# Two norms joined at a border, a reordered end, and low parts of split weights behind the attention steps of their mark

## The chip, the cores and the metric

The kernel runs on one core of one Trainium2 chip. The metric is device time in microseconds, here the median of three runs; a profiled execution of the same kernel gives the trace.

## What is computed

A transformer block of two layers is followed by a second block with its own weights. All of it works on 256 rows of 1024 fp32 values. Cut to what matters:

```
def first_block(x, mem, ...):                       # two layers
    for layer in range(2):
        h = rms_norm(x, norm_g[layer])
        proj = h @ w_in[layer]                      # heads of three kinds: sb, mb, mem
        ...                                         # attention of each kind, gated by silu
        mixed = concat([o_sb, o_mb, o_mem])
        x = x + mixed @ w_out[layer]                # "wo"
    return rms_norm(x, final_norm_g)                # the final norm of the first block

def second_block(x, meta_tokens, ...):
    h = concat([filler, meta, x])                   # 16 meta rows ahead of the 256
    u = rms_norm_2(h, pre_mix_gain)
    proj = u @ w_in_2                               # qa, ka, va, qb, kb, vb, gates
    o_swa  = windowed_gqa_sink_attention(...)       # 16 heads in 4 groups: "swa"
    o_diff = differential_attention(...)            # 8 heads: "diff"
    merged = g_swa * (o_swa @ w_branch_swa) + g_diff * (o_diff @ w_branch_diff)
    h = h + rms_norm_2(merged @ w_out, post_mix_gain)
    u = rms_norm_2(h, pre_ffn_gain)
    f = (silu(u @ w_gate) * (u @ w_up)) @ w_ffn_out
    return (h + rms_norm_2(f, post_ffn_gain))[128:]
```

At the border between the blocks two norms follow each other on the same rows: the final norm makes x, and the first norm of the second block makes its input xn of that x.

## The kernel before

**Tiling.** The 256 rows are two tiles, t=0 and t=1, of 128. A weight matrix is worked through in units: a unit is two chunks of 128 rows of the matrix by 512 columns (384 in swa and diff). For precision each fp32 operand is split into a high and a low part, and a unit does for each tile and chunk three matmuls: high x high, high x low, low x high. So a unit is six matmuls for t=0 (step `unit`) and six for t=1 (`unit_end`). Four units make a group, and each tile of a group adds up in one bank of PSUM.

**Weights.** SyncE loads a unit's raw weights into one of four raw buffers. ScalarE writes the high part (w_hi), VectorE the low part (w_lo = raw - w_hi). Both are one step, `split`, in the old kernel. A raw buffer is free, and its next load goes out, when its low part is written. The parts go into one of five slots (ten late in the kernel). A split is put into the order when the unit is less than SPLIT_AHEAD = 3 units ahead of the one that TensorE begins, and the slot's last user has ended.

**The order.** All engines walk one list of steps, STEPS, and each issues its own part of every step; semaphores hold them together. `make_plan` writes a timeline of units, norms and turns (transposes on TensorE), and `lay_out` makes the list of it. When the last unit of a head group has ended, the group's attention steps are put at marks, so many units later, by the table SLOTS: the key and query turns (turn_qk), scores, the softmax (soft), scale (VectorE divides the probabilities of a pair of heads by their sum; this is L1802), turn_p and turn_tm (transposes of the probabilities), out_t (times the values), mix_t (split of the result). A mark is half a unit. At each mark stand the matmuls of the half unit, the evacuation of a finished bank, the split (by kind of group ahead of or behind the attention steps) and the attention steps due. For head groups of swa and diff GpSimd rotates queries and keys (rope, L1128 to L1140) before turn_qk. Two small banks of PSUM are shared in a ring by turns and outs, so a turn or out can wait until the result of two turns ago has been read.

**The splits of turned operands.** A turn's result in PSUM is copied by ScalarE into a high part (h_hi, m_hi, mix_hi) and VectorE subtracts it into the low part (h_lo, m_lo, mix_lo, L1717 and L1807). The operand is ready with the low part.

**The border to swa.** After the last units of wo of layer 1 (a[3] and b[3] for the two halves of the columns) VectorE adds the bank to x. Then comes `norm` for x to x (the final norm) and `norm` for x to xn: each is ScalarE's square over 1024 columns with a sum (L1496), a logarithm and an exponential, and VectorE's scaling of the row by that and by the gain (L1706). xn is turned into h for t=0 and, after three units of swa, for t=1. Between them TensorE does a `meta` group: 8 chunks of weights meta_w with 16 meta rows (L1202). Its weights are loaded whole (two DMAs of 1 MB, L1017) when the meta group before has been read.

**The end.** After the last hidden group of the ffn, its product f is turned (turn_f) and split into m_hi and m_lo. ScalarE has to load another table of functions (`tables`, L1549) before the last norm. Four held units of w_ffn_out run for t=0 first, then the two last units, which need the new m_hi and m_lo.

## Time and profile before

| | |
|---|---|
| runs | 833.49, 833.73, 832.29 us |
| median | 833.49 us |
| the profiled execution | 831.91 us |
| its span, first to last instruction | 830.1 us |
| mean granted clock of TensorE | 0.995 |
| TensorE busy | 801.1 us, 97% |
| VectorE, ScalarE, GpSimd busy | 497.9, 467.8, 136.5 us |

A row of the timeline gives the start in us from the start of the span, the duration, the engine, the line, what is written and what is read, and in brackets the idle time just before and the engine that ended it. Matmuls are pipelined: one starts before the one in front of it has ended, so the distance of starts says what a matmul costs.

### The profile page before, as it was taken

The page shows a single profiled execution, that of the slowest core. Times are in us where ns is not written, and L with a number is a line of the kernel's source. Part 1 is how long each engine was busy: PE and PEld are TensorE (multiplying, and loading weights), DVE is VectorE, ACT ScalarE, POOL GpSimd, SP SyncE. Part 2 cuts the span into 40 slices and gives each one's busy share as a digit, 9 for nine tenths or more (in the row PEclk, how much of TensorE's full clock was granted, in tenths as well). Part 3 has the DMA queues.
Part 4 walks back from the last instruction along what each step waited for, and adds up shares of the span by engine and source line. Part 5 has one row for each costly group of instructions (what it writes and reads, how often), then busy time and mean ns, then how long its engine had stood idle before and what let it go on. Part 6 is the DMA issues. An engine that isn't in the chain of part 4 may idle for free.

```text
span 830.1 us, 12690 instructions
## 1 busy us (share of the span) xinstructions
PE 801.1 (97%) x4238; PEld 651.3 (78%) x4238; DVE 497.9 (60%) x731; ACT 467.8 (56%) x1004; POOL 136.5 (16%) x204
## 2 busy tenths in 40 slices
PE   7999999999999998899999999999999999999996
PEld 5887778887777885877778888778887888888885
DVE  5456565684566555666765767666787544555454
ACT  5677586475666555555566565654557433444352
POOL 2011021000243110434433546000000000000000
PEclk9999999999999999999999999999999999999999
DMA  8964553469764546442323435456775645465631
GB/s 237 285 174 145 151 169 104 144 190 286 228 203 128 190 152 197 138 123 85 89 77 96 128 116 164 128 178 228 244 230 160 203 151 179 153 203 191 209 133 51
DMA packets 147294, 137.78 MB, mean 166 GB/s; under 512 B 15024, under 2 KB 115648, under 8 KB 147232
## 3 DMA queue, kind: packets, MB, share of 16 engines
q1 hardware_dynamic: 145136, 129.89, 50.9%
q0 software_dynamic: 2096, 7.09, 3.1%
q8 instruction: 36, 0.59, 0.3%
q14 instruction: 26, 0.21, 0.1%
HBM read 135.90 MB, written 1.05 MB: 165 GB/s over the span
## 4 chain that ended last, share of the span: by engine, by line
PE 82%; ACT 5%; DVE 5%; POOL 4%; issue 3%; DMA 1%; DVEq 0%; SPq 0%; ACTq 0%; POOLq 0%
PE psum L1182 66%; PE psum L1160 7%; PE psum L1281 3%; PE psum L1416 3%; ACT w_hi L1463 2%; ACT probs L1590 1%; POOL rtmp L1128 1%; POOL rtmp L1130 1%; DVE w_lo L1659 1%; DVE probs L1802 1%; PE psum L1202 1%; POOL rtmp L1132 1%; PE psum L1342 1%; POOL stage L1134 1%; PE psum L1384 1%
## 5 line engine op out<-in xcount | busy, mean ns | idle before, releaser
L1659 DVE TENSOR_TENSOR w_lo<-raw,w_hi 128x1024 fp32r<-128x1024 f32 (+1 forms) x234 | 274.1, 1194 | 118.8 <-ACT w_hi L1463 83.4
L1182 PE MATMUL psum<-w_hi,h_hi 128*128 128x512 f32 (+1 forms) x656 | 259.9, 396 | 4.8 <-DVE w_lo L1659 2.2
L1463 ACT ACTIVATE w_hi<-raw 128x1024 fp32r<-128x1024 f32 (+1 forms) x234 | 230.9, 1011 | 41.0 <-PE psum L1182 17.2
L1182 PE MATMUL psum<-w_lo,h_hi 128*128 128x512 f32 (+1 forms) x656 | 247.2, 377 | 0.0
L1182 PE MATMUL psum<-w_hi,h_lo 128*128 128x512 f32 (+1 forms) x656 | 246.6, 376 | 0.0
L1182 PEld LDWEIGHTS psum<-w_hi,h_hi 128*128 128x128 f32 x656 | 124.1, 189 | 31.4 <-issue 14.8
L1182 PEld LDWEIGHTS psum<-w_lo,h_hi 128*128 128x128 f32 x656 | 123.9, 189 | 19.2
L1182 PEld LDWEIGHTS psum<-w_hi,h_lo 128*128 128x128 f32 x656 | 124.3, 190 | 15.4
L1182 PE MATMUL psum<-w_hi,m_hi 128*128 128x512 f32 x152 | 60.3, 397 | 1.2 <-DVE m_lo L1717 1.2
L1182 PE MATMUL psum<-w_lo,m_hi 128*128 128x512 f32 x152 | 59.3, 390 | 0.0
L1182 PE MATMUL psum<-w_hi,m_lo 128*128 128x512 f32 x152 | 59.2, 389 | 0.0
L1128 POOL TENSOR_TENSOR rtmp<-stage,cf 128x256 f32<-128x256 f32 (+2 forms) x36 | 30.3, 840 | 160.5 <-ACT stage L1525 128.7
L1182 PE MATMUL psum<-w_hi,mix_hi 128*128 128x512 f32 x128 | 52.9, 414 | 0.0
L1590 ACT ACTIVATE probs<-psum,stats 128x272 f32<-128x272 f32 (+2 forms) x104 | 47.1, 465 | 10.5 <-DVE stats L1787 6.0
L1182 PE MATMUL psum<-w_lo,mix_hi 128*128 128x512 f32 x128 | 50.2, 392 | 0.0
L1182 PE MATMUL psum<-w_hi,mix_lo 128*128 128x512 f32 x128 | 49.9, 390 | 0.0
L1505 ACT ACTIVATE m_hi<-psum 128x512 fp32r<-128x512 f32 (+1 forms) x27 | 14.4, 536 | 62.1 <-PE psum L1160 62.1
L1717 DVE TENSOR_TENSOR m_lo<-psum,m_hi 128x512 fp32r<-128x512 f32 (+1 forms) x27 | 16.4, 609 | 51.4 <-ACT m_hi L1505 51.4
L1608 ACT ACTIVATE p_t<-psum 128x512 f32<-128x512 f32 (+1 forms) x44 | 24.1, 566 | 27.8 <-PE psum L1160 27.7
L1518 ACT ACTIVATE stage<-psum 128x128 f32<-128x128 f32 (+1 forms) x52 | 15.6, 301 | 37.5 <-PE psum L1182 37.5
L1160 PE MATMUL psum<-cf,probs 128*128 128x128 f32 (+1 forms) x212 | 30.7, 274 | 4.1 <-DVE probs L1802 2.5
L1182 PEld LDWEIGHTS psum<-w_hi,m_hi 128*128 128x128 f32 x152 | 28.6, 188 | 7.1 <-issue 1.6
(171 smaller groups left out, 1001.1 us busy)
## 6 DMA issues: line engine op xcount, KB each, us to landing
raw<-in_w_in SPq DMA_DIRECT2D x112, 256.0 KB, 3.8
raw<-in_w_ffn_in SPq DMA_DIRECT2D x88, 256.0 KB, 4.1
raw<-in_w_in SPq DMA_DIRECT2D x24, 512.0 KB, 3.9
raw<-in_w_out SPq DMA_DIRECT2D x24, 512.0 KB, 3.5
raw<-in_w_in SPq DMA_DIRECT2D x64, 192.0 KB, 2.7
raw<-in_w_ffn_out SPq DMA_DIRECT2D x22, 512.0 KB, 4.2
meta_w<-in_w_in SPq DMA_DIRECT2D x10, 1024.0 KB, 7.9
raw<-in_w_mem_kv SPq DMA_DIRECT2D x8, 512.0 KB, 3.9
```

The source lines that it names most:

```text
L1128: nc.gpsimd.tensor_tensor(a, v[:, t, :, 0:w], ct[:, t].unsqueeze(1).to_broadcast(shape), ALU.mult)
L1160: last = nc.tensor.transpose(o, i, cf[0:n, C_ID:C_ID + n])
L1182: last = nc.tensor.matmul(psum[:, bank, 0:n], sx[name][:, c, t * P:(t + 1) * P], wx[:, kk, 0:n], start=u["first"] and kk == 0 and z == 0, ...
L1281: return nc.tensor.matmul(o, l, r, start=start, stop=stop, skip_group_check=True)
L1416: last = nc.tensor.matmul(dst, src[:, blk * P:(blk + 1) * P], vs[:, kt, v0:v0 + wide], start=(n == 0), stop=end)
L1463: nc.scalar.activation(weights(u)[0][:, :, 0:n], raw[:, u["raw"], :, 0:n], ACT.Copy)\
L1505: nc.scalar.activation(dst[0], src, ACT.Copy).then_inc(turned_hi, 1)
L1518: nc.scalar.activation(st[:, t, 0:K["qw"]], ps[:, 0:K["qw"]], ACT.Copy, scale=SCALE)
L1590: last = nc.scalar.activation(probs[:, j % 4, t, 0:n], src, ACT.Exp, bias=stt[:, t:t + 1], accum_out=stt[:, 2 + t:3 + t])
L1608: last = nc.scalar.activation(p_t[:, s["pt"] % 2, 0:n], psum[:, s["bank"], 0:n], ACT.Copy)
L1659: nc.vector.tensor_tensor(lo[:, :, 0:n], raw[:, u["raw"], :, 0:n], hi[:, :, 0:n].bitcast(F32), ALU.subtract)\
L1717: nc.vector.tensor_tensor(dst[1], src, dst[0].bitcast(F32), ALU.subtract).then_inc(turned, 1)
```

## The change

**Joined norms.** At the border the two norms become one chain. With y = x * gain of the final norm, X = mean(x^2) and Y = mean(y^2), the two factors multiply to (Y + eps (X + eps))^-1/2. The new steps: `row_scale` (VectorE writes y by halves of 512 columns into xn), `row_sum` (ScalarE squares a half of x and a half of y with their sums), `twin` (GpSimd adds the sums of x and makes the bias, ScalarE does one logarithm and one exponential, VectorE scales y by that and the second gain, in two halves, each with its own signal to the turns). x itself, the result of the final norm, is needed only much later; its two scalings now stand behind the fourth swa group.

**Meta weights** are loaded and waited for by halves, the first half as soon as the first four chunks of the group before were read; the meta group at the border is done in two halves around the first turn.

**swa's first group** has marks of its own, SLOTS["swa0"]: scores and softmax of its second pair half a unit later than in the other groups (6.95 for 6.45), and all that follows them too; turn_p of the first pair stays at 6.5. Its units for t=0 run all four before t=1 is turned.

**Low parts** are a step of their own, `split_lo`, which stands behind the attention steps of the mark in which the high part is made. High parts keep their places.

**The end**: one high part and the table load stand behind turn_f.

```diff
     "swa": dict(turn_qk=(3.25, 2.75), scores=(4.45, 4.45, 6.45, 6.45), soft=(4.95, 4.95, 6.95, 6.95),
...
+    "swa0": dict(turn_qk=(3.25, 2.75), scores=(4.45, 4.45, 6.95, 6.95), soft=(4.95, 4.95, 7.45, 7.45),
+                 scale=(5.95, 8.45), turn_p=(6.5, 6.5, 9, 9), turn_tm=(6.9, 9.4), out_t=(7.5, 10),
...
         while split < min(most, held) and split < begun + ahead and order[split]["before"] < ended:
             steps.append(("split", order[split]))
+            lows.append(order[split])
             split += 1
+
+    def low_parts(most):
+
+        while len(lows) > most:
+            steps.append(("split_lo", lows.popleft()))
...
         for k in sorted(k for k in due if k <= clock):
             steps.extend(due.pop(k))
         if g["kind"] in SPLIT_LAST:
+            low_parts(0)
             splits()
+        else:
+            low_parts(0)
...
         else:
-            final, after = norm(source="x", dest="x"), norm(source="x", dest="xn")
-            line.append(final[0])
-            line.extend(("unit_b", u) for u in (a[3], b[3]))
-
+            final, after = norm(source="x", dest="x", twin=True), norm("twin", source="x", dest="xn")
             metas.append(meta_group(4))
             metas[4]["evac_later"] = True
-            line.extend([after[0], ("meta", metas[4]), final[1]])
-            line.extend(norm_turns("xn", "h", 0))
-            line.append(after[1])
+            for us, g in ((a, outs[0]), (b, outs[1])):
+                line.extend([("unit_a", us[3]), row_scale(final, g, 0), row_sum(final, g, 0, "x"),
+                             row_sum(final, g, 0, "y")])
+            line.append(("hold", "begun"))
+            turns = norm_turns("xn", "h", 0)
+            line.extend([("unit_b", a[3]), row_scale(final, outs[0], 1), after[0], row_sum(final, outs[0], 1, "x")])
+            line.extend([("unit_b", b[3]), ("meta", metas[4], (0, KC // 2)), turns[0]])
+            line.extend([row_sum(final, outs[0], 1, "y"), row_scale(final, outs[1], 1)])
+            line.extend([("meta", metas[4], (KC // 2, KC)), ("hold", None), ("splits", "one"), ("hold", "begun"), turns[1]])
+            line.extend([row_sum(final, outs[1], 1, "x"), row_sum(final, outs[1], 1, "y"), after[1]])
...
         if kv == 0:
-            line.extend(("unit_a", u) for u in g["units"][:3])
-            line.extend(norm_turns("xn", "h", 1))
-            line.append(("unit_a", g["units"][3]))
-            line.extend(("evac", dict(g=metas[n], t=0)) for n in (3, 4))
-            line.extend(("unit_b", u) for u in g["units"])
+            us = g["units"]
+            us[3]["evac_later"] = True
+            line.extend(("unit_a", u) for u in us)
+            line.extend(norm_turns("xn", "h", 1) + [("evac", dict(g=g, t=0)), ("hold", None), ("splits", "one")])
...
+        elif kv == 3:
+            add(g)
+            line.extend(final)
...
-    line.append(("tables", None))
     held = outs_of(nf - 3) + outs_of(nf - 2)
-    line.extend(("unit_a", u) for u in held[:3])
-    line.append(("turn_f", dict(j=nf - 1, f=last_g)))
-    line.append(("unit_a", held[3]))
+    line.extend(("unit_a", u) for u in held[:2])
+    line.extend([("hold", "begun"), ("unit_a", held[2]), ("turn_f", dict(j=nf - 1, f=last_g))])
+    line.extend([("hold", None), ("splits", "one"), ("tables", None), ("unit_a", held[3])])
...
                     for i in range(2):
+                        if g["n"]:
+
+                            sp.wait_ge((meta_first, meta_done)[i], g["n"])
                         src = cols[i * 4 * P:(i + 1) * 4 * P, :].rearrange("(k p) n -> p k n", p=P)
-                        sp.dma_start(meta_w[:, 4 * i:4 * i + 4, :], src).then_inc(meta_landed, 16)
+                        sp.dma_start(meta_w[:, 4 * i:4 * i + 4, :], src).then_inc(meta_landed[i], 16)
...
+                elif what == "twin":
+                    N, t = s["norm"], s["t"]
+                    c = 4 * (N["n"] % 4) + 2 * t
+                    Y1 = hsum[:, 7 + 4 * t:8 + 4 * t]
+                    rs = nstat[:, 16 + c:17 + c]
+                    act.wait_ge(row_bias, t + 1)
+                    act.wait_ge(row_summed, 4 * t + 4)
+                    link(nc.scalar.activation(rs, Y1, ACT.Ln, bias=twins[:, t:t + 1]))
+                    nc.scalar.activation(rs, rs, ACT.Exp, scale=-0.5).then_inc(rstd_ready, 1)
```

What it moves, at three places. First VectorE at the border, from the addition of the first wo half to x up to the low parts of h for t=1. Before:

```order
L1878 TENSOR_TENSOR x<-x,psum 128x512
L1659 TENSOR_TENSOR w_lo<-raw,w_hi 128x2x384
L1878 TENSOR_TENSOR x<-x,psum 128x512
L1659 TENSOR_TENSOR w_lo<-raw,w_hi 128x2x384
L1706 SCALAR_TENSOR_TENSOR x<-x,nstat,gain 128x1024
L1878 TENSOR_TENSOR x<-x,psum 128x512 x2
L1706 SCALAR_TENSOR_TENSOR xn<-x,nstat,gain 128x1024
L1706 SCALAR_TENSOR_TENSOR x<-x,nstat,gain 128x1024
L1717 TENSOR_TENSOR h_lo<-psum,h_hi 128x4x128 x2
L1706 SCALAR_TENSOR_TENSOR xn<-x,nstat,gain 128x1024
```

Now, from the low parts of two swa units on:

```order
L1764 TENSOR_TENSOR w_lo<-raw,w_hi 128x2x384 x2
L2001 TENSOR_TENSOR x<-x,psum 128x512
L1805 TENSOR_TENSOR xn<-x,gain 128x512
L2001 TENSOR_TENSOR x<-x,psum 128x512
L1805 TENSOR_TENSOR xn<-x,gain 128x512
L2001 TENSOR_TENSOR x<-x,psum 128x512
L1805 TENSOR_TENSOR xn<-x,gain 128x512
L1814 SCALAR_TENSOR_TENSOR xn<-xn,nstat,gain 128x512 x2
L2001 TENSOR_TENSOR x<-x,psum 128x512
L1840 TENSOR_TENSOR h_lo<-psum,h_hi 128x4x128
L1805 TENSOR_TENSOR xn<-x,gain 128x512
L1764 TENSOR_TENSOR w_lo<-raw,w_hi 128x2x384
```

The whole-row scalings in a chain are gone; each half of x is followed at once by its product with the gain, and xn of t=0 is scaled in two halves before the last half of x is even added.

Second TensorE in the third swa group's units, where the first group's attention lies: qk and cb are the scores of its second pair, "cf,probs 128x128" is turn_p of the first, "cf,probs 16x128" turn_tm. Before:

```order
L1281 MATMUL psum<-qk 128x272 x4
L1281 MATMUL psum<-cb 128x128 x4
L1160 MATMUL psum<-cf,probs 128x128 x8
...
L1160 MATMUL psum<-cf,stage 128x128 x2
L1160 MATMUL psum<-cf,gates 128x16
L1160 MATMUL psum<-cf,probs 16x128 x4
```

Now:

```order
L1229 MATMUL psum<-cf,probs 128x128 x8
...
L1229 MATMUL psum<-cf,stage 128x128 x2
L1229 MATMUL psum<-cf,gates 128x16
L1229 MATMUL psum<-cf,probs 16x128 x4
L1353 MATMUL psum<-qk 128x272 x4
L1353 MATMUL psum<-cb 128x128 x4
```

The scores moved behind six matmuls of a unit and two turns, and turn_p is now the first of them.

Third VectorE in the head group mb 1 of layer 0, where o_st is the result of a mem head. Before:

```order
L1717 TENSOR_TENSOR m_lo<-psum,m_hi 128x4x128
L1659 TENSOR_TENSOR w_lo<-raw,w_hi 128x1024
L1835 RECIPROCAL rec<-stats 128x2
L1844 SCALAR_TENSOR_TENSOR o_st<-psum,rec,sgate 128x64 x2
L1717 TENSOR_TENSOR m_lo<-psum,m_hi 128x4x128
```

Now:

```order
L1840 TENSOR_TENSOR m_lo<-psum,m_hi 128x4x128
L1958 RECIPROCAL rec<-stats 128x2
L1967 SCALAR_TENSOR_TENSOR o_st<-psum,rec,sgate 128x64 x2
L1764 TENSOR_TENSOR w_lo<-raw,w_hi 128x1024
L1840 TENSOR_TENSOR m_lo<-psum,m_hi 128x4x128
```

The low part went behind the result of the head and in front of the next low part of a turned operand.

## Rows read from the trace of the kernel before

**Rows 1.** The page: its first line and TensorE's busy time.

```profile
span 830.1 us, 12690 instructions
...
PE 801.1 (97%) x4238; PEld 651.3 (78%) x4238; DVE 497.9 (60%) x731; ACT 467.8 (56%) x1004; POOL 136.5 (16%) x204
```

**Rows 2.** TensorE's waits by releaser: us in total, times, longest.

```profile
PE psum L1160 <- DVE probs L1802: 2.5, 6, 1.0
...
PE psum L1160 <- DVE o_st L1844: 1.5, 2, 1.2
```

**Rows 3.** Timeline of TensorE at the border.

```profile
320.76 0.47 PE L1182 MATMUL psum<-w_hi,mix_hi 128*128 128x512 f32 x1
...
328.77 1.91 PE L1202 MATMUL psum<-meta_w,meta_s 128*16 128x512 f32 x16 [2.29 <-DMA meta_w<-in_w_in]
331.42 1.06 PE L1160 MATMUL psum<-cf,xn 128*128 128x128 f32 x8 [0.73 <-DVE xn L1706]
333.73 0.41 PE L1182 MATMUL psum<-w_hi,h_hi 128*128 128x384 f32 x1 [1.25 <-DVE h_lo L1717]
...
338.49 1.04 PE L1160 MATMUL psum<-cf,xn 128*128 128x128 f32 x8
...
340.70 0.41 PE L1182 MATMUL psum<-w_hi,h_hi 128*128 128x384 f32 x1
```

**Rows 4.** Stretches: busy us (instructions) per engine, then granted clock.

```profile
334.00:337.50 3.50, 3.50 (x13) 3.50 (x12) 2.70 (x4) 2.17 (x6) 0.55 (x2) 0.51 0.49 154
341.00:346.00 5.00, 5.00 (x31) 5.00 (x30) 4.15 (x8) 3.63 (x8) 2.89 (x5) 1.00 0.32 83
```

**Rows 5.** Meta weights: the group before's first matmuls, the DMA issues, their landing.

```profile
318.32 1.05 PE L1202 MATMUL psum<-meta_w,meta_s 128*16 128x512 f32 x8
...
L1017 SPq DMA_DIRECT2D meta_w<-in_w_in x2: 368/438/509, 320.8 to 321.2; - x2
...
DMA to landing us min/median/max: 5.2/6.4/7.5
```

**Rows 6.** Groups of VectorE by form (busy, mean ns), and a square in ScalarE's timeline.

```profile
L1878 DVE TENSOR_TENSOR x<-x,psum 128x512 f32<-128x512 f32 x8 | 5.3, 683 | 3.7 <-PE psum L1182 3.7
...
L1706 DVE SCALAR_TENSOR_TENSOR x<-x,nstat,gain 128x1024 f32<-128x1024 f32 x2 | 2.6, 1284 | 1.3 <-ACT nstat L1499 1.3
...
814.57 0.60 ACT L1474 ACTIVATE p_t<-psum 128x512 f32<-128x512 f32 x1 [3.59 <-PE psum L1182]
```

**Rows 7.** Timelines of GpSimd, VectorE and TensorE around swa's first rope.

```profile
345.83 4.39 POOL L1128 TENSOR_TENSOR rtmp<-stage,cf 128x320 f32<-128x320 f32 x1 [1.78 <-ACT stage L1521]
...
345.94 3.54 DVE L1659 TENSOR_TENSOR w_lo<-raw,w_hi 128x768 fp32r<-128x768 f32 x4
...
352.54 0.44 PE L1160 MATMUL psum<-cf,stage 128*128 128x128 f32 x2 [1.13 <-POOL stage L1140]
```

**Rows 8.** Timeline of TensorE: second scores and first turn_p of swa.

```profile
363.82 1.19 PE L1281 MATMUL psum<-qk 64*128 64x272 f32 x8 [1.20 <-ACT stats L1594]
...
365.56 1.06 PE L1160 MATMUL psum<-cf,probs 128*128 128x128 f32 x8 [0.22 <-DVE probs L1802]
```

**Rows 9.** Timelines of VectorE and TensorE in two head groups of layer 0.

```profile
137.75 1.23 DVE L1659 TENSOR_TENSOR w_lo<-raw,w_hi 128x1024 fp32r<-128x1024 f32 x1 [3.85 <-ACT w_hi L1463]
...
72.13 0.85 PE L1416 MATMUL psum<-stage,probs 128*128 128x64 f32 x6 [0.55 <-DVE m_lo L1717]
```

**Rows 10.** Timeline of TensorE: the last turn_p of a group's second pair.

```profile
433.60 1.06 PE L1160 MATMUL psum<-cf,probs 128*128 128x128 f32 x8 [0.95 <-DVE probs L1802]
```

**Rows 11.** Timelines of TensorE and ScalarE at the end.

```profile
812.93 0.47 PE L1182 MATMUL psum<-w_hi,m_hi 128*128 128x512 f32 x1 [1.21 <-DVE m_lo L1717]
...
806.24 1.28 ACT L1549 ACT_TABLE_LOAD   x1
807.54 2.96 ACT L1463 ACTIVATE w_hi<-raw 128x1024 fp32r<-128x1024 f32 x3
810.40 0.57 ACT L1505 ACTIVATE m_hi<-psum 128x512 fp32r<-128x512 f32 x1
```

More of the change, by code:

```diff
@@ L196, in lay_out @@
     free, user = deque(range(NSLOT)), {}
-    for what, arg in timeline:
+    for what, arg, *_ in timeline:
         if what == "more_slots":
@@ L240, in part @@
         if g["kind"] in SPLIT_LAST:
+            low_parts(0)
             splits()
-    for what, arg in timeline:
+        else:
+            low_parts(0)
+    for what, arg, *rows in timeline:
         if what == "splits":
-            splits(split + 1 if arg == "one" else arg)
+            splits({None: len(order), "one": split + 1}.get(arg, arg))
+            low_parts(0)
         elif what == "hold":
@@ L276, in lay_out @@
             steps.append((what, arg))
-    assert not due and begun == ended == split == len(order)
+    assert not due and not lows and begun == ended == split == len(order)
     return steps
```

125 lines of the change are left out of this document (106 added, 19 removed).

## Prediction

> **What bounds the kernel now.** I read the page first. TensorE is busy for 801.1 of 830.1 us [rows 1], so no edit that leaves its matmuls alone can return more than the 29 us in which it is idle, plus what its clock lost. The change keeps every matmul; it moves them and what feeds them. So the question at each place is which wait of TensorE ends last there. The profiled execution took 831.91 us, 1.8 over its span, and is 1.6 below the median of the runs, 833.49; I make the sum against 831.91 and add 1.6 at the end.
>
> The waits of TensorE by releaser come next: no single one is large. The longest sum is 2.5 us in 6 waits for VectorE's scaled probabilities; another is 1.5 in 2 for o_st [rows 2]. The timeline of TensorE shows where the others lie. At the border to swa (from the last wo matmul, which ends at 328.77 - 2.29 = 326.48, to the first t=1 matmul of swa at 340.70) it waits 2.29 us for meta weights, 0.73 for xn and 1.25 for h_lo [rows 3], 4.27 us in all. Behind these waits the granted clock is 0.51 for 3.5 us, which is the lower of its two levels, 1.2 GHz [rows 4]. Work that ran 3.5 us there would have taken 3.5 x 0.51 = 1.8 at 2.4 GHz, so 1.7 us more are lost. The matmul counts agree: 13 in 3.5 us against 31 in 5.0. The border loses 6.0 of its 14.2 us.
>
> **The border.** Three things are done to it. *Meta weights:* two DMAs were issued at 320.8 and 321.2 and landed 5.2 and 7.5 us later, at 326.0 and 328.7 [rows 5]; the matmuls waited for both. Now each half waits only for its own readers and has its own semaphore. The first four matmuls of group 3 end at 318.32 + 1.05 = 319.4 [rows 5], so half 0 can go out at about 319.6 and land by 325, and half 1 still goes out at about 320.8, behind a queue 1 us shorter, and lands at about 327.4. The four matmuls of half 0 take half of 1.91 [rows 3], from 326.5 to 327.4, and do not wait.
>
> *Joined norms:* before, ScalarE's square and its two small steps, VectorE's scaling of x, and the same again for xn ran one behind the other. Now the squares of x and of x*gain are summed by halves while the last wo units run. VectorE adds a half to x in 0.683 [rows 6]; the product with the gain has no row, and I take 0.65 for it, between half a low part, which also has two SBUF inputs (1.23 for 1024, so 0.62 [rows 9]), and a scaling of a whole row, 1.28 [rows 6]. ScalarE's square of 512 is 0.60 [rows 6]; with its sum read out behind it I take 0.7. The chain for t=0: the four half units from 320.76 to 326.48 [rows 3] are 1.4 apart, so a's half leaves TensorE at 322.2 and b's at 323.6; a's is in x at 323.3 (two low parts are now queued in front of it) and b's at 324.6, and the four squares end at about 326.1. GpSimd's three 128x1 operations have no row: from nothing, under the last square, to 4.39 if one is locked out like the rope's [rows 7]; I take 0.7, ending at 326.3, since they are far smaller than that. Logarithm and exponential end at 326.9, and the first half of xn is there at 327.6. TensorE gets there at 327.4: it waits 0.2 to 0.5, and again nothing for the second half, which lies under meta's second four matmuls. h_lo of the first half is ready near 329.5, as the turns end near 329.6; the 1.25 is gone. Without gaps of that length the clock should hold.
>
> *What is late next:* t=1. Its turns now stand behind all four swa units of t=0, with only themselves as cover. Before, 2.2 us passed from the start of the turns (338.49) to the first t=1 matmul (340.70) [rows 3], and a unit of 6 matmuls at 0.17 (1.0 us) lay inside; now nothing does, so about 1.1 us of new wait. Border: 6.0 - 0.3 - 1.1 = **4.6 us** gained; from 2 (half 1 late and the clock down again) to 5.7.
>
> **swa's first head group.** *Rope:* GpSimd's multiply took 4.39 us while VectorE ran four low parts of 3.54 in a row, and TensorE then waited 1.13 for the rope's copy [rows 7]. The four are now spread: three stand before the first meta sum, two between the two sums and one behind. The cover from the last swa unit to this turn stays three units. I take **0.9** of the 1.13, with 0 and 1.13 as ends. The Trainium skill (SBUF — State Buffer, section "SBUF: two separate sides") says that a VectorE operation with two SBUF inputs and a GpSimd operation that reads SBUF lock each other out for a whole instruction; by that rule two low parts in a row cost the rope 1.8 us, and if they stay in its way this term is 0. The row of 4.39 beside 3.54 agrees with it.
>
> *Scores and turn_p:* before, the second pair's scores waited 1.20 for the first pair's softmax, ran 1.7, and turn_p then waited 0.22 for the scaled probabilities [rows 8]. The new slot 6.95 puts the scores half a unit behind, but turn_p keeps 6.5 and comes first. It needs the scaling, which ended at about 365.4 and does not depend on those scores. TensorE reaches it at 363.82 - 1.20 = 362.6. So it waits up to 365.5 - 362.6 = 2.9, less about 0.6 since the maximum no longer stands behind a low part: 2.3 in place of 1.42. The scores then wait for nothing. That is **-0.8**; +1.1 if the chain to the scaling were shortened as far, -1.5 at worst.
>
> *Final norm of x:* its two VectorE operations, 1.284 each [rows 6], move behind the mark of the last swa group, between mix_lo and the next maximum. They delay that softmax by up to 2.57. How much of it TensorE sees depends on the slack of this chain, which has no row: its turn_p waits are 0.2 to 1.0 before [rows 2], so there is none at its end, but matmuls of two units lie in it. I take a third, **-0.8**, with 0 and -2.57 as ends. Its six small ScalarE operations I cost at nothing, since ScalarE waits there for TensorE's transposes; without that cover they cost up to 0.3 each, half of a 512 square [rows 6].
>
> **Low parts behind the steps of their mark.** A low part takes 1.23 us with 1024 columns. Where one stood in front of a step that TensorE waits for, the wait goes: 1.5 in two waits for o_st [rows 2], the longer, 1.2, behind the w_lo at 137.75 [rows 9]; 0.95 at 433.60 [rows 10], where I count 0.9; and half of the other five waits for the probabilities (2.5 - 0.95 = 1.55), those of the groups' first pairs, 0.8. Where the part now comes in front of something else, a wait grows: at 72.13 TensorE waits 0.55 for m_lo [rows 9], and a low part now runs in front of that m_lo: -1.1. In layer 0 the norm of mem and the turn of the memory keys get a low part in front of them in the same way; TensorE waits for both already, and I count 0.4 each. Sum: 1.5 + 0.9 + 0.8 - 1.1 - 0.8 = **+1.3**. Waits that now are just covered and will show can't be read from the trace; I leave them to the range (-3 to +1). I cost late low parts at nothing for the matmuls: none of the waits here is for w_lo, two or three units are split ahead, and a part moves by less than a half unit.
>
> **The end.** TensorE reaches the units that need m_lo at 812.93 - 1.21 = 811.7 and waits 1.21. ScalarE had put a table load (1.28) and three high parts (2.96, up to 810.5) in front of m_hi, which ran from 810.40 for 0.57 [rows 11]; VectorE made the third low part behind the third high part, to about 812.1, and m_lo behind that. Now table load and third high part are behind m_hi. The turn has ended by 810.4, so m_hi ends at 811.0 or before and m_lo, as long as a sum of 512 at 0.683 [rows 6], at 811.7. The third high part ends at 812.0 and its low part at 813.2; the unit that wants it comes one half unit, 1.4, behind 811.7. So at most 0.1 is left at each: **+1.1**, from 0.6 to 1.2. The table load ends at about 813.3, as the first square is due, which has the whole of t=1 as cover.
>
> **Sum:** 4.6 + 0.9 - 0.8 - 0.8 + 1.3 + 1.1 = 6.3 us. 831.91 - 6.3 = 825.6, and with 1.6 for the median **827.2 us**.
>
> **Rivals.** (1) *The border gives half.* Half 1 of meta shares the wires with three weight loads and lands at 329, the gaps add up and the clock falls again: border 2.3, time 829.5, range 829 to 831. For: before, the fall came at 334 behind gaps like these; against: there they were 4.27 us. Chance 0.17. (2) *swa0 and the low parts help everywhere,* as they are meant to: +1.1 instead of -0.8, final norm free, 1 more from low parts: 6.3 + 1.9 + 0.8 + 0.5 = 9.5, 824.0, range 821.5 to 825. Chance 0.18. (3) *Slower.* Low parts pushed in front of turned parts, as at 72.13, cost 1.1 at each such mark. I count one for certain; the sum turns at 6.3/1.1, some 6 more such marks in the head groups of both layers, and by 9 of them the time is 833.5 + 3 = 837. Chance 0.07. For: layers 0 and 1 have 14 head groups with the same steps; against: most turned parts there aren't waited for at all now. (4) *No change:* new waits at three or four marks eat the border, 833. Chance 0.08.
>
> **How the numbers follow.** My forecast, 825 to 829, has 0.50. A measurement of this kernel tells about 0.2%, 1.7 us, from no change. Faster by more: forecast, (1) and (2), 0.85; within: 0.08; slower: 0.07. Leaving out (3), most of (4) and the low edge of (2) keeps 0.8 within 822.5 to 831.5.
>
> **What would show it.** Right: no wait for meta_w, the clock at 1.00 from 334 on, a wait for h_lo of about 1 us at the first t=1 unit of swa; a wait for the probabilities of about 2.3 us at the first turn_p of swa; none over 0.3 for o_st, at the place of 433.60 and at that of 812.93; about 1.6 at that of 72.13. Wrong: a wait for meta_w over 1 us or a clock of 0.5 in the border; waits for m_lo, mix_lo or sbt in more than three head groups.

## Result and profile after

The changed kernel took 834.42 us in the median of 20 runs (832.76 to 835.93), the kernel before 833.11 (830.69 to 834.03, also 20 runs). The ratio is 1.0022, with an interval of 1.0015 to 1.0029: slower by 0.2% (1.3 us by the medians, 1.8 by the ratio), where 6.3 us of gain had been forecast and 822.5 was the low, 831.5 the high end of the range. The profiled execution spans 832.4 us, against 830.1 in [rows 1]:

```profile
span 832.4 us, 12731 instructions
...
PE 800.0 (96%) x4238; PEld 650.4 (78%) x4238; DVE 501.5 (60%) x737; ACT 469.7 (56%) x1014; POOL 137.4 (17%) x210
```

TensorE's waits by releaser (us in total, times, longest), which answer to [rows 2], say where to look. The scaled probabilities were 2.5 us in six waits and are 4.4 in four; the blended ones of diff (L1945) and p_t are new, and m_lo in front of L1488 has grown from 0.5:

```profile
PE psum L1229 <- DVE probs L1925: 4.4, 4, 2.4
PE psum L1229 <- DVE probs L1945: 3.1, 5, 1.5
...
PE psum L1229 <- ACT p_t L1713: 2.2, 1, 2.2
...
PE psum L1488 <- DVE m_lo L1840: 1.7, 1, 1.7
```

**The border** did what it was made for, though less of it. No wait for meta_w is left, and the granted clock is 1.00 in the stretches of [rows 4], where it was 0.51 in the first. What answers to the three waits of [rows 3] is one for xn and, one tile later, one for h_lo. TensorE's timeline and the stretches:

```profile
328.30 0.63 PE L1229 MATMUL psum<-cf,xn 128*128 128x128 f32 x4 [1.22 <-DVE xn L1814]
...
337.12 0.41 PE L1251 MATMUL psum<-w_hi,h_hi 128*128 128x384 f32 x1 [1.17 <-DVE h_lo L1840]
```

```profile
334.00:337.50 3.50, 2.33 (x17) 2.09 (x16) 2.24 (x4) 1.96 (x5) 0.94 (x2) 1.00 0.42 122
341.00:346.00 5.00, 5.00 (x31) 5.00 (x30) 4.89 (x6) 3.46 (x6) 3.93 (x5) 1.00 0.73 192
```

**Swa's first head group.** TensorE's timeline, where [rows 8] had 1.20 and 0.22, and ScalarE's ahead of the second wait:

```profile
360.73 1.06 PE L1229 MATMUL psum<-cf,probs 128*128 128x128 f32 x8 [2.38 <-DVE probs L1925]
...
377.62 0.60 PE L1229 MATMUL psum<-cf,probs 128*16 128x128 f32 x4 [2.24 <-ACT p_t L1713]
```

```profile
374.92 0.49 ACT L1695 ACTIVATE probs<-psum,stats 128x272 f32<-128x272 f32 x1 [3.88 <-DVE stats L1897]
...
376.97 1.09 ACT L1713 ACTIVATE p_t<-psum 128x512 f32<-128x512 f32 x2
```

The first wait is the forecast 2.3. The second nobody had priced: the copy of the second pair's turned probabilities (p_t) now stands on ScalarE behind the four exponentials of the next group, which run from 374.92 on.

**Swa's fourth group.** VectorE runs the two scalings of x in front of the maximum (the reduction, L1891), and TensorE waits twice:

```profile
393.44 3.09 DVE L1829 SCALAR_TENSOR_TENSOR x<-x,nstat,gain 128x1024 f32<-128x1024 f32 x2
...
396.46 1.28 DVE L1891 TENSOR_REDUCE stats<-psum 128x4 f32<-128x1088 f32 x1
```

```profile
401.60 1.19 PE L1353 MATMUL psum<-qk 64*128 64x272 f32 x8 [0.91 <-ACT stats L1699]
...
404.68 1.94 PE L1229 MATMUL psum<-cf,probs 128*128 128x128 f32 x8 [1.56 <-DVE probs L1925]
```

The eight transposes at 404.68 take 1.94 us, where they take 1.06 at 360.73. The stretches say why (the granted clock is the figure in front of the last two): 1.00 behind the wait of 2.38, and 0.50, the lower level, behind these two.

```profile
360.00:363.00 3.00, 2.27 (x17) 2.10 (x17) 2.32 (x3) 1.40 (x3) 0.00 (x0) 1.00 0.17 43
...
404.00:407.00 3.00, 2.32 (x10) 2.35 (x11) 2.86 (x5) 0.94 (x2) 0.00 (x0) 0.50 0.22 77
```

**Low parts.** In layer 0 the wait of 0.55 in [rows 9] is 1.66, with a low part in front of m_lo, as forecast. In diff a low part stands in front of the reciprocals with which the blended probabilities begin, and its neighbours on VectorE and TensorE are:

```profile
71.36 1.22 DVE L1764 TENSOR_TENSOR w_lo<-raw,w_hi 128x1024 fp32r<-128x1024 f32 x1
...
73.33 0.85 PE L1488 MATMUL psum<-stage,probs 128*128 128x64 f32 x6 [1.66 <-DVE m_lo L1840]
```

```profile
510.19 1.22 DVE L1764 TENSOR_TENSOR w_lo<-raw,w_hi 128x1024 fp32r<-128x1024 f32 x1
...
512.51 1.62 DVE L1945 SCALAR_TENSOR_TENSOR probs<-probs,rec 128x272 f32<-128x272 f32 x2
...
514.28 0.84 PE L1229 MATMUL psum<-cf,probs 128*128 128x128 f32 x6 [1.47 <-DVE probs L1945]
```

**The end.** The wait of 1.21 in [rows 11] is gone; m_lo is there before the unit that wants it:

```profile
814.18 0.69 DVE L1840 TENSOR_TENSOR m_lo<-psum,m_hi 128x512 fp32r<-128x512 f32 x1 [1.37 <-ACT m_hi L1610]
...
815.02 0.47 PE L1251 MATMUL psum<-w_hi,m_hi 128*128 128x512 f32 x1
```

**Where the time went.** Both kernels issue 2808 matmuls with split weights. I number them in order and compare when the same number starts in the two traces; a step in the difference is a gain or loss at that place. In us, minus is a gain:

| place | forecast | traced |
|---|---|---|
| start (up to 25 us) | 0 | -0.3 |
| layer 0: 62.8, 73.3, 95.6 | +1.9 | +0.4 +1.1 +0.4 |
| layer 0: 130 | 0 | +0.4 |
| o_st waits, layers 0 and 1 | -1.5 | -1.4 -1.0 |
| border | -4.6 | -3.2 |
| rope of swa's first group | -0.9 | -0.7 |
| first group, first pair | +0.8 | +0.5 |
| first group, second pair | 0 | +2.2 |
| fourth group (final norm) | +0.8 | +3.4 |
| the other swa turns, up to the last | -1.7 | -1.6 |
| diff | 0 | +2.3 |
| gates and after | 0 | +0.7 |
| end | -1.1 | -1.1 |
| sum | -6.3 | +2.1 |

The spans differ by 2.3. Of diff's 2.3, 0.6 (a wait of 0.87 at 486.58) is in no other trace with these low parts. A trace is one execution: the same order of instructions starts up to 1 us earlier or later in another, and the clock can fall at another place (see the last section), so a step of this table is firm where a second trace repeats it.

### The profile page after: what moved, and what is told of

The parts are those of the page before. It is cut to its first block, busy times and chain, and to the rows that moved or that the text cites. A ratio compares the mean times of both kernels' runs of the same rounds, so it can differ in the third digit from the quotient of the medians.

```text
span 832.4 us, 12731 instructions
## 1 busy us (share of the span) xinstructions
PE 800.0 (96%) x4238; PEld 650.4 (78%) x4238; DVE 501.5 (60%) x737; ACT 469.7 (56%) x1014; POOL 137.4 (17%) x210
## 4 chain that ended last, share of the span: by engine, by line
PE 87%; DVE 5%; ACT 4%; issue 3%; DMA 1%; SPq 0%; POOL 0%; ACTq 0%; DVEq 0%; POOLq 0%
PE psum L1251 68%; PE psum L1229 7%; PE psum L1353 4%; PE psum L1488 3%; DVE w_lo L1764 2%; PE psum L1456 1%; ACT w_hi L1535 1%; PE psum L1414 1%; PE psum L1272 1%; ACT probs L1695 1%; DMA gain<-in_norm_g 1%; DVE probs L1925 0%; PE psum L1491 0%; DMA raw<-in_w_in 0%; PE psum L1416 0%
## 5 line engine op out<-in xcount | busy, mean ns | idle before, releaser
L1229 PEld LDWEIGHTS psum<-cf,probs 128*128 128x128 f32 (+1 forms) x212 | 23.4, 133 | 16.1 <-issue 10.1
```

The lines of the kernel that those rows point to most:

```text
L1229: last = nc.tensor.transpose(o, i, cf[0:n, C_ID:C_ID + n])
```

## The experiments

All ratios are to the kernel before, which ran on the same chip beside it. The changed kernel's own is 1.0022. The difference of two such ratios is uncertain by 1 to 1.6 us, so a difference near 1 us needs the trace beside it.

**Each part undone.** First the low parts, right behind their high parts again:

```diff
-            lows.append(order[split])
+            steps.append(("split_lo", order[split]))
```

> The changed kernel, with each low part back right behind its high part; all else as changed. Theory 1 (losses at single places): the low parts' move cost 0.4 + 1.1 + 0.4 us in layer 0 (waits at 62.8, 73.3, 95.6), about 2.3 in diff (waits for the blended probabilities, up to 1.47 at 514.28) and 1.0 in the four gates groups, and gave 1.4 at the o_st wait of layer 0, 0.5 in layer 1 and 1.5 in the last swa attention. Undone, the sum is about 1.7 us less than the changed kernel: 832.7, and the wait at the fourth turn of probabilities in diff falls from 1.47 to under 0.2. Theory 2 (the low parts are the whole loss): 829 or below, with the waits around swa's first and last head groups gone too. Theory 3 (swa's attention chain is the bound there, and the 4 us won at the border are waited off again whatever the order): 832 to 834, and waits in swa grow by what goes elsewhere.

Measured: 1.0076 (1.0060 to 1.0092), 4.5 us slower than the changed kernel instead of 1.7 faster. Outside swa each place came back about as named: 0.4, 1.1, 0.4 and 0.4 us regained in layer 0, 1.4 and, in layer 1, 0.9 lost at and behind o_st, the wait of 1.47 in diff gone. In swa it lost 3.5 us at the first turn of probabilities and 1.3 at the third:

```profile
353.29 1.44 DVE L1764 TENSOR_TENSOR w_lo<-raw,w_hi 128x768 fp32r<-128x768 f32 x1 [1.66 <-ACT w_hi L1535]
...
354.65 1.28 DVE L1891 TENSOR_REDUCE stats<-psum 128x4 f32<-128x1088 f32 x1
```

```profile
361.83 1.94 PE L1229 MATMUL psum<-cf,probs 128*128 128x128 f32 x8 [3.22 <-DVE probs L1925]
...
378.28 1.07 PE L1229 MATMUL psum<-cf,probs 128*128 128x128 f32 x8 [1.46 <-DVE probs L1925]
```

With a low part in front of the maximum the wait is 3.22 instead of 2.38. That is 0.8 of the 3.5; the rest is the clock, which is at the lower level from 361 to 367:

```profile
361.00:364.00 3.00, 2.17 (x10) 2.20 (x11) 2.43 (x3) 1.20 (x3) 0.00 (x0) 0.50 0.06 16
364.00:367.00 3.00, 3.00 (x13) 2.16 (x11) 0.44 (x1) 0.41 (x1) 0.00 (x0) 0.50 0.85 244
```

So theory 1 held at the places that it named, but its sum did not, since it had left out swa's first group; theory 2 fell. With swa's new marks the low parts' move keeps the maximum free. How much of the clock's 2.7 us every execution pays is not shown: the spans of the six runs go from 834.0 to 837.9 us.

Second, swa's first group on the common marks:

```diff
-    for what, places in SLOTS["swa0" if g.get("kv") == 0 else g["kind"]].items():
+    for what, places in SLOTS[g["kind"]].items():
```

> The changed kernel, with swa's first head group on the marks of the other swa groups (second pair at 6.45 again, all behind it half a unit earlier). Theory 1: the wait of 2.38 us for the first turned probabilities becomes one of about 1.4 at the scores and the turn together, and the wait of 2.24 us of the second pair's turn for ScalarE's copy of the transposed probabilities goes: 3 us less, 831.4. Theory 2 (low parts): no more than 0.5 us. Theory 3 (the chain is the bound): the 2.24 goes but the next turn of probabilities waits as much more; no change, 834.

Measured: 0.9979 (0.9970 to 0.9989), 3.6 us less than the changed kernel. The scores wait 0.64 and the turn 0.22; the wait for p_t is gone:

```profile
360.73 1.19 PE L1353 MATMUL psum<-qk 64*128 64x272 f32 x8 [0.64 <-ACT stats L1699]
...
362.46 1.06 PE L1229 MATMUL psum<-cf,probs 128*128 128x128 f32 x8 [0.22 <-DVE probs L1925]
```

Theory 1 stands, theory 3 falls: nothing behind waited longer.

Third, the final norm of x taken out of swa:

```diff
-        elif kv == 3:
-            add(g)
-            line.extend(final)
...
-        add(pl.group("bswa", ...))
+        us = pl.group("bswa", ...)["units"]
+        line.extend([("unit_a", us[0]), final[n], ("unit_b", us[0])])
+        line.extend(("unit", u) for u in us[1:])
```

> The changed kernel, with the two scalings of x by the final norm moved from behind swa's fourth group to the two branch groups bswa, one each, behind a half unit in which ScalarE and VectorE stand idle. Theory 1: the waits of 0.91 for stats and 1.56 for the probabilities at 401 to 405 us and the lower clock behind them (0.83 over 400 to 410) go, and nothing new waits in bswa: 3.4 us less, 831.0. Theory 2: no more than 0.5. Theory 3: waits in swa's second half stay at 2 us or more; 834.

Measured: 0.9983 (0.9970 to 0.9995), 3.2 us less than the changed kernel; 4.0 at this place in the trace, where both waits at the fourth group are gone and the clock is 1.00 from 400 to 410 (0.83 in the changed kernel). Theory 1 stands.

Fourth, the old end:

> The changed kernel with the old end (table load and all three high parts in front of the last turn of the ffn's product). All theories: the wait of 1.2 us for m_lo in front of the last units comes back, 1.1 us more, 835.5. If the end's gain is only moved to the tail, no change.

Measured: 1.0036 (1.0021 to 1.0051), 1.2 us more, which by itself is within the noise; but the wait of 1.21 for m_lo is back at 814.58, and the trace loses 1.0 us there and no more behind it. The term of the end was right.

**One part alone.** The border, with everything else of before (final norm in the bswa groups):

> The border done alone: the joined norms, the order of meta and of swa's first units, and the halves of the meta weights; the low parts, swa's first marks and the end are as before, and the final norm of x stands in the two bswa groups, where it cost nothing. Theory 1 (single places): the border gains 3.9 us by the trace of the changed kernel, and nothing is given back, so the ratio to the kernel before is 0.9953. Rival (given back): with the low parts in front of the attention steps, TensorE comes 4 us early to a chain of VectorE that is no earlier, and waits at the first head group's scores or probabilities for 2 us or more: 0.998 to 1.

Measured: 0.9961 (0.9948 to 0.9973), 3.2 us. The gain at the border is not given back in swa. The trace has 3.8 us up to 355 and loses 1.0 of them at a new wait in bswa: the final norm does cost something there, against what was expected. It comes up again below.

The low parts alone:

> The low parts' move done alone, with the old border, the old marks and the old end (the meta weights' halves have their own signals). By single places read from the changed kernel's trace: layer 0 loses 0.4 + 1.1 + 0.4 + 0.4 and gains 1.4, layer 1 gains 0.5 to 0.8, the swa attention gains 1.0 to 1.6, diff loses about 1.7 and gates 1.0. Sum: 1.2 to 1.6 us slower, ratio 1.0015 to 1.002. If the move is worth in the old order what it was worth in the changed one (5.0 us), it is 0.994.

Measured: 1.0003 (0.9988 to 1.0018). In the old order their move is worth nothing that can be told, and the gains and losses of the table come back (layer 0 the same four, diff +1.3 at one turn, the last turn of swa -1.0). The trace also loses 2.1 us at swa's first rope, with a wait of 1.77 for GpSimd (1.13 before) and a clock of 0.50 from 353 to 356; m_border_old below, which has the same order up to there, waits 1.07 and keeps the clock, so I don't count that as a price of the low parts. Their worth of 4.5 us in the changed kernel is for the most part worth against the new marks.

The old border in the changed kernel (the final norm stands at the border again, as it did):

> The changed kernel with the old border (two norms one behind the other, meta in one piece, swa's first units in the old order); low parts, swa's first marks and the end as changed. If the border is worth in the changed kernel what it is worth alone (0.9961 against the kernel before, 3.2 us), this one is 3.2 us above the changed one: ratio to the kernel before 1.006. If the border's gain was given back in swa, because TensorE came early to a chain that was no earlier, it is within 1 us of the changed kernel: 1.001 to 1.0035.

Measured: 1.0033 (1.0015 to 1.0051). I had overlooked that this also takes the norm out of swa. The trace shows both: 3.5 us lost at the border and the rope, 4.0 regained at the fourth group. As a package, the joined norms with the scalings put off into swa bring nothing that can be told (1.0033 against 1.0022, with intervals that overlap), while the border alone, with the scalings in bswa, brings 3.2.

**The two waits of the first group told apart:**

```diff
-scale=(5.95, 8.45), turn_p=(6.5, 6.5, 9, 9), turn_tm=(6.9, 9.4)
+scale=(5.95, 8.45), turn_p=(6.97, 6.97, 9, 9), turn_tm=(6.98, 9.4)
```

> The changed kernel with the first pair's turned probabilities of swa's first head group behind the second pair's scores, at the same mark (they stood in front of them); the second pair's marks stay. It tells the two waits of this group apart. Theory 1: the wait of 2.38 us falls to about 1, as 1.3 us of scores and six matmuls lie under it, and the wait of 2.24 us for ScalarE's copy stays whole, since the second pair's softmax is still half a unit late: 1.2 us less than the changed kernel. Rival: both waits are one chain and the second shrinks too, 3 us less.

Measured: 1.0035 (1.0021 to 1.0049), no gain. The first wait fell as expected, and the second grew:

```profile
362.27 1.09 PE L1229 MATMUL psum<-cf,probs 128*128 128x128 f32 x8 [1.07 <-DVE qk L1853]
...
375.92 0.61 PE L1229 MATMUL psum<-cf,probs 128*16 128x128 f32 x4 [2.73 <-ACT p_t L1713]
```

By the count of weight matmuls 1.7 us are won up to the second wait and 2.0 lost at and behind it. Neither expectation had it. Of the 2.0 only 0.5 is the longer wait, 2.73 for 2.24: ScalarE's exponentials, on which it hangs, began 1.7 us earlier too (373.21 for 374.92; this trace starts 0.4 earlier), so that chain followed TensorE for the most part. The other 1.5 is the clock, which stayed at 1.00 behind the wait of 2.24 and is at its lower level for a part of these two stretches behind that of 2.73:

```profile
376.00:379.00 3.00, 3.00 (x16) 2.12 (x18) 1.75 (x4) 2.25 (x4) 0.00 (x0) 0.67 0.20 58
379.00:382.00 3.00, 3.00 (x18) 1.70 (x16) 1.17 (x2) 0.38 (x1) 0.00 (x0) 0.77 0.44 131
```

The mean clock of the five runs is 0.993, that of the changed kernel's twenty 0.995, so on the whole it was lower in them; that the longer wait is the reason is not shown.

**The cures.** Low parts behind the attention steps only where that helped, the common marks, the norm in bswa:

```diff
             lows.append(order[split])
+            if not late:
+                low_parts(0)
...
+        late = g["kind"] in ("mb", "mem") and begun > 24 or g["kind"] == "swa" or g.get("d", 9) < 2
```

> All the cures together: the changed kernel with swa's first group on the old marks, the final norm of x in the bswa groups, and the low parts behind the attention steps only where that helped (swa, the first two diff groups, and the mb and mem groups but for the first), right behind their high parts elsewhere. Theory 1, by places: 3.0 less for the marks, 2.8 to 3.4 for the norm, 2.2 in layer 0, 1.9 in diff and 1.0 in gates less: 11 us below the changed kernel, ratio to the kernel before 0.989. If gains are given back down the line, 0.994 or more.

Measured: 823.09 us, against 831.18 for the kernel before beside it, ratio 0.9898 (0.9885 to 0.9912); by the ratios that is 10.3 us below the changed kernel, where 11 had been expected. It beats both. The sum over places held, with misses both ways: the marks and the norm gave 3.8 and 3.9 in the trace, layer 0 gave 1.4 for 2.2, and a new wait (below) cost 1.1.

The first of the edits alone, in the changed kernel:

> The changed kernel with one edit: low parts behind the attention steps only in swa, the first two diff groups, and the mb and mem groups but for the first; right behind their high parts elsewhere. By the single places 2.2 us in layer 0, 1.5 to 1.9 in diff and 1.0 in gates come back: 4.4 to 5.1 us below the changed kernel, ratio to the kernel before 0.9965 to 0.9970. If what is won early is waited off at swa, whose marks are unchanged here, ratio 1.000 or more.

Measured: 0.9979 (0.9969 to 0.9989), 3.6 us, some 1 less than expected. Diff and gates came back about as named (1.7 and 0.9). Of the 2.2 in layer 0 the trace has 1.3: the three places of the table gave 1.9, the fourth kept its wait of 0.2, and TensorE waits for o_st again, 0.36 at 142.62, which costs 0.6. And the clock fell at other places, behind the waits of 2.38 and of 2.24, which are as long as in the changed kernel, and held behind those of 0.92 and 1.56:

```profile
361.00:364.00 3.00, 3.00 (x16) 1.88 (x16) 0.44 (x1) 0.70 (x2) 0.00 (x0) 0.61 0.84 244
...
378.00:381.00 3.00, 3.00 (x16) 2.28 (x16) 2.48 (x4) 1.57 (x3) 0.00 (x0) 0.60 0.13 37
...
402.00:406.00 4.00, 1.95 (x16) 1.47 (x17) 2.55 (x5) 1.35 (x5) 0.00 (x0) 1.00 0.71 229
```

By the count of matmuls each fall costs 1.3 to 1.5 us (+1.5 and +1.3 against the changed kernel, and -1.3 at the fourth group). Two falls in place of one make this execution slower, but they don't explain the missing 1 us of the median: the mean clock of the eleven runs is 0.995, as in the changed kernel's twenty, and that of the profiled one 0.993. What layer 0 did not give back is about as much as is missing.

**Why the fourth group cost 4 us.** The same two scalings one unit later, behind the group's softmax:

```diff
-        elif kv == 3:
-            add(g)
-            line.extend(final)
...
-        add(pl.group("diff", ...))
+        us = pl.group("diff", ...)["units"]
+        line.extend([("unit", us[0])] + (final if d == 0 else []))
+        line.extend(("unit", u) for u in us[1:])
```

> The changed kernel with one edit: the final norm's two scalings of x stand one unit later, behind the softmax of swa's fourth group (in the changed kernel they are in front of its maximum). Work and amount are the same. Place theory: what cost 4.0 us was that 3.1 us of VectorE stood in front of the maximum, from which scores, exponentials, scaling and turn hang. Here their factors come behind the group's exponentials on ScalarE (about 400) and the two scalings end near 403.2, 1.1 us behind the time at which the probabilities' scaling began before: the turn waits about 1.3 us in all, the scores not at all, and 2.7 us of the 4.0 come back: ratio to the kernel before 0.999. Amount theory (VectorE has no room for 2.6 us in swa, wherever): 3 us or more are lost again, ratio 1.002.

Measured: 1.0013 (1.0004 to 1.0023), 0.7 us less than the changed kernel, which is within the noise; the trace regains 0.5 of the 4.0 us at this place. That number is the amount theory's (3 us or more lost again, 1.002) and not the place theory's (2.7 back, 0.999).

```profile
398.45 2.48 DVE L1828 SCALAR_TENSOR_TENSOR x<-x,nstat,gain 128x1024 f32<-128x1024 f32 x2 [2.54 <-ACT nstat L1587]
```

```profile
403.02 1.94 PE L1228 MATMUL psum<-cf,probs 128*128 128x128 f32 x8 [1.82 <-DVE probs L1924]
```

But VectorE stood idle for 2.54 us ahead of the scalings, waiting for factors that ScalarE makes behind the exponentials, so it did have room for them and the amount theory's reason does not hold either. In their new place they stand in front of the probabilities' scaling, again in the chain maximum, exponential, scaling, turn. One wait of 1.82 took the place of 0.91 and 1.56, and the clock fell as before (0.83 from 400 to 410). The place theory had said a wait of 1.3 and had left out the clock, which make up its miss. What the runs show is that the scalings cost 3.3 to 4.0 us by the traces at either place in this chain, against c_norm_late, where they stand outside of it.

**The wait of 0.84 us in the cured kernel.** GpSimd's, VectorE's and TensorE's timelines of h_sel at the rotation of the last diff head:

```profile
509.60 1.47 DVE L1831 SCALAR_TENSOR_TENSOR x<-x,nstat,gain 128x1024 f32<-128x1024 f32 x1
...
509.95 1.44 POOL L1203 TENSOR_TENSOR rtmp<-stage,cf 128x128 f32<-128x128 f32 x1
...
512.25 0.44 PE L1231 MATMUL psum<-cf,stage 128*128 128x128 f32 x2 [0.84 <-POOL stage L1205]
```

> All cures, with the final norm's first scaling moved once more, from the first bswa group, where GpSimd still rotates the last diff head (its multiply took 1.44 us beside the scaling, 0.46 to 0.65 without it, and TensorE then waited 0.84 for it), to the second, and the second scaling to the first gates group; no rotation runs there. Expected: the wait of 0.84 goes to about 0.2, 0.7 to 0.9 us less than with both in the bswa groups: ratio to the kernel before 0.989. If the operation of VectorE was not what slowed GpSimd, no change: 0.9898.

Measured: 0.9942 (0.9930 to 0.9954), 3.7 us slower than h_sel. The 0.84 went, but a wait nobody had in mind came: the second scaling, which ends at 544.9, holds the buffer of the gain, the gates' bias is loaded into it only then (issued at 545.43, landed 5.1 us later), and TensorE waits for the first gates bank.

```profile
551.42 0.47 PE L1253 MATMUL psum<-w_hi,h_hi 128*128 128x512 f32 x1 [3.63 <-DVE gates L2006]
```

> As h_sel (ratio 0.9898), with both scalings of x in the second bswa group, one unit apart: behind the last rotation, and in front of the gates, so that the buffer of the gain is free in time for the gates' bias (in the gates group it was not: TensorE waited 3.6 us). Expected: the wait of 0.84 for the rotated head goes, and no wait for the bias: 0.8 us less than h_sel, ratio 0.9889. If VectorE's scaling isn't what slows the rotation: 0.9898.

Measured: 823.84 us, 0.9894 (0.9878 to 0.9911), the same as h_sel. The 0.84 is gone here too, and no wait for the bias came; instead the second scaling delays the blended probabilities, for 1.2 us:

```profile
534.59 0.85 PE L1231 MATMUL psum<-cf,probs 128*128 128x128 f32 x6 [0.63 <-DVE probs L1947]
...
536.33 0.47 PE L1253 MATMUL psum<-w_hi,h_hi 128*128 128x512 f32 x1 [0.89 <-DVE xn L2010]
```

**The wait for xn.** One swap at the border, on top of h2_norm_later:

```diff
-row_scale(final, outs[0], 1), after[0], row_sum(final, outs[0], 1, "x")])
+after[0], row_scale(final, outs[0], 1), row_sum(final, outs[0], 1, "x")])
```

> As the run before, and at the border VectorE's product for the first half of t=1 stands behind the scaling of xn for t=0 instead of in front. In the changed kernel's trace this product (325.94 to 326.63) ran beside GpSimd's last addition for the bias, which took 0.70 us where the two others took 0.2, and the chain to xn waited for it; TensorE waits 1.22 us for xn. Expected: the addition takes 0.2, the wait falls by 0.5 to about 0.7, 0.5 us less: ratio 0.9884. If the product costs as much in its new place (the next low parts of h behind it), no change.

Measured: 0.9943 (0.9929 to 0.9956), as without it (0.9942; the 0.9884 expected was reckoned before h2_norm_later had missed). GpSimd's addition took 0.19 and the wait for xn fell by 0.5 as expected, and 0.37 came for h_lo, as the second alternative had it:

```profile
326.65 0.63 PE L1231 MATMUL psum<-cf,xn 128*128 128x128 f32 x4 [0.68 <-DVE xn L1816]
...
329.22 0.41 PE L1253 MATMUL psum<-w_hi,h_hi 128*128 128x384 f32 x1 [0.37 <-DVE h_lo L1842]
```

## Why the prediction was wrong

The terms that rested on a wait seen in the trace of before had the right sign, and most of them the right size. Those for work put into a place where nothing waited yet did not, and they are all on the losing side: the final norm of x, swa's second pair and the waits that were "just covered" are 7.2 us off together, of 8.4 in all. The step that failed is to price such work at nothing or at a third.

**The border** (4.6 said, 3.2 traced). The mechanism was right: no wait for meta_w, no low clock. The size was off by 1.4. The chain to xn was the step: TensorE waited 1.22 us for it instead of 0.2 to 0.5. "GpSimd's three 128x1 operations" were taken as 0.7 us; they took 0.20, 0.19 and 0.70 one after another, each with its way to the next, and ended at 326.7 instead of 326.3, and TensorE came 0.3 earlier than forecast (327.1). The wait of about 1.1 for h_lo at t=1 was forecast and is 1.17. Some 0.4 of the 1.4 lies in no wait and stays open.

**Swa's first marks** (0.8 said, 2.7 traced). The first pair's wait was right (2.3 said, 2.38 measured). What I did not do is to follow the second pair: I priced the slot of its scores and not the marks of all that follows them, though the change names them. Its turn_p moved half a unit, past the softmax of the next group, and on ScalarE the copy of p_t then stands behind four exponentials. The order lists would have shown it. b_swa0_old, which puts the common marks back, is 3.6 us faster.

**The final norm of x** (0.8 said, 3.4 traced). "I take a third" was the failed step, and c_norm_late shows what it was worth (3.2 us). The two operations lasted 3.09 us and not 2.57, since GpSimd rotated beside them, and the chain behind them had no slack: TensorE waited 0.91 + 1.56 against 0.28 before, 2.2 us more, and the lower clock added 1.3 (from n_sel, where the same waits without it cost that much less). Even the end of the range that I gave, 2.57, was too small, since it priced the delay and not the clock.

**Low parts** (gain of 1.3 said, loss of 1.3 traced). The named places were right to 0.2 us, the o_st wait of layer 0 and those of [rows 9] and [rows 10] among them, but for layer 1: its o_st wait was 0.3, and 1.0 was gained at and behind it. A wait that was not named, in layer 0, cost 0.4. But "waits that now are just covered" was left to the range. They are 1.7 us in diff, where the part went from in front of m_lo, which nobody waits for, to in front of the blended probabilities, and 0.7 in the gates groups, where it went between the two evacuations of a bank. This is rival (3)'s mechanism, and other steps than the turned parts that it names. It also left out what the move is good for: with swa's new marks it keeps the wait of 2.38 from being one of 3.22 and the clock from falling there (a_lo_old is 4.5 us slower in all; the fall is seen in one execution).

**The end** (1.1 said, 1.1 traced, 1.2 by the run that undoes it) and **the rope** (0.9 said, 0.7 traced) held.

**Slips in the sums**, which change little: 2.3 in place of 1.42 is 0.9 and not 0.8; the scores' "1.7" includes the wait of 0.22; that wait is counted in the 1.42 and again among the five other waits of the low parts; rival (2) speaks of 1 more from low parts and adds 0.5.

**Rivals.** None was it. I gave the border half (1) and all help (2) more than a third of the chance and slower 0.07, with a single mechanism. The range missed because its upper end, 831.5, lay beside that of rival (1), which halves one term. The low ends that I had given to the six terms (2, 0, -1.5, -2.57, 1.3 - 3 and 0.6) add up to a loss of 3.2 us: that sum should have stood beside the chance of 0.07.

## What to carry to other kernels

When a step moves in an in-order kernel, list for each engine what it passes and what now stands behind it, through the whole chain, and price each new neighbour at its full time until a row shows slack; zero is the best case, and a wait seen before is only where the gains are. Where a chain such as maximum, exponential, scaling and turn is already waited for at its end, any operation put into it costs most of its time, wherever in the chain it is put, and the clock may fall behind the longer wait. When an edit shortens one wait and brings nothing in all, look at the next one in both traces: how much longer it is, and what the granted clock is behind it. In f_turnp7 the first was 0.5 us and the second 1.5.

## What the runs showed of the hardware

**GpSimd beside VectorE.** An addition of 128x1 on GpSimd takes 0.19 us; the one that ran beside VectorE's product of two SBUF inputs took 0.70. GpSimd's and VectorE's timelines of the changed kernel:

```profile
325.72 0.19 POOL L1139 TENSOR_SCALAR eps_col<-eps_col 128x1 f32<-128x1 f32 x1
325.99 0.70 POOL L1140 TENSOR_TENSOR eps_col<-eps_col,hsum 128x1 f32<-128x1 f32 x1
```

```profile
325.94 0.69 DVE L1805 TENSOR_TENSOR xn<-x,gain 128x512 f32<-128x512 f32 x1
```

It ended when VectorE's did, at 326.7. The rotation's multiplies of 128x128 took 0.45 to 0.66 in most places of the changed kernel, 1.17 to 1.27 in ten that ran beside a low part, and 1.44 in h_sel beside the scaling of x. So the expectation of h2_norm_later had only the short ones in view. It goes the other way as well: the two operations on the blended probabilities took 1.62 at 512.51 and 1.47 at 484.96 (in front of the wait of 0.87) with GpSimd rotating, 0.91 elsewhere. The Trainium skill (SBUF — State Buffer, section "SBUF: two separate sides") says that the one that comes second is blocked for the whole instruction of the other; the 0.70 that ends with VectorE's 0.69 agrees with it, and shows that it holds for an operation of one column too.

**The clock.** In the changed kernel the granted clock stayed at 2.4 GHz behind a wait of 2.38 us and one of 2.24, and fell to 1.2 behind waits of 0.91 and 1.56 that lie three microseconds apart. In n_sel, whose waits at these three places are the same to 0.01, it fell at the first two and held at the third. So the length of a wait did not tell in these runs whether the clock would fall. Nor did the order of the instructions: on TensorE it is the same in b_swa0_old as in the changed kernel up to 360 us, and both wait 1.66 us for m_lo in layer 0 (73.33 and 73.42). The stretch behind that wait, in the changed kernel and in b_swa0_old:

```profile
74.00:76.00 2.00, 2.00 (x13) 1.66 (x13) 1.42 (x2) 0.86 (x2) 1.74 (x3) 1.00 0.69 239
```

```profile
74.00:76.00 2.00, 2.00 (x10) 1.57 (x10) 1.43 (x2) 0.32 (x1) 1.83 (x4) 0.65 0.70 240
```

The six other traces with this wait (c_norm_late, d_end_old, l_lows, m_border_old, f_turnp7, c2_norm_diff0) keep 1.00 there. Behind the 0.91 and 1.56 it fell in four traces of five. A fall is thus in part a matter of the single execution, and one trace each cannot show that an edit caused or cured it; the twelve runs of c_norm_late went from 828.7 us at a mean clock of 0.998 to 832.1 at 0.994. A fall cost 1.3 to 1.6 us, and the lower clock 2.7 behind the wait of 3.22 in a_lo_old: about as much as the waits themselves, and in none of my terms behind the border.
